# Routed experts in units of 32 rows in four column lanes, with the gate weights copied by ScalarE, in place of units of 64 rows in two lanes

## The chip, the cores and the metric

The kernel runs on one core of one Trainium2 chip. The metric is the device time of one execution in microseconds (us); the lower the better. TensorE is written PE, VectorE DVE, ScalarE ACT, GpSimd POOL, and SP is the engine that issues most DMAs. All tensors are 32-bit floats.

## The reference

One layer of a decoder: 256 prompt tokens and 64 sample tokens pass a native-sparse-attention block with a gating unit, a memory cross-attention and, last, a mixture of experts, whose part is what the change touches:

```python
def hier_moe(h, w_rg, w_re, w_gate, w_up, w_down):     # h: 320 tokens x 2048
    pg = softmax(xf @ w_rg); g_top = argmax(pg)        # one of 4 groups
    fl = (xf @ w_re)[group g_top]; pf = softmax(fl)    # 4 experts of that group
    top_p, top_i = top_k(pf, 2)                        # two experts per token
    wts = top_p / sum(top_p) * max(pg)
    act = silu(xf @ w_gate[e]) * (xf @ w_up[e])        # 2048 -> 512, each of 16 experts
    act = act * comb[:, e]                             # weight of expert e for the token, or 0
    return sum over e of act @ w_down[e]               # 512 -> 2048
x = x + hier_moe(rmsnorm(x, g_moe_norm), ...);  y = rmsnorm(x, g_final)
```

Every expert has three weight matrices of 4.19 MB (gate, up, down); the 16 experts have 201 MB. 320 tokens with two experts each are 640 pairs. The reference's router, evaluated on the reference's own inputs, gives experts 0 to 15 these numbers of pairs: 15, 38, 32, 51, 86, 64, 52, 30, 44, 62, 77, 29, 4, 20, 15, 21. In units of 64 rows that is 18 units (experts 4 and 10 have two, all others one). In units of 32 rows it is 26: experts 4 and 10 have three, experts 1, 3, 5, 6, 8 and 9 two, the other eight one.

## The kernel before

The program is a sequence of stages, each a block in which all engines run their own instruction lists and meet at semaphores. The last block is the expert stage (line 2408 on). Just before it, a short block (line 2239) makes the routing table on DVE: how many units there are, which expert each has, and which token stands in each row of it.

The expert stage is a loop over units, called turns. In one turn PE

- turns the rows of the next unit, which POOL has gathered from memory with an indirect DMA (`turn_rows`, L2473);
- multiplies this unit's activation with the down weights (`down`, transposes L2510, matmuls L2517: 16 matmuls of 512 columns);
- multiplies the next unit's rows with gate and up weights (`gate_up`, L2499 and L2500: 16 chunks of 128 input features; gate fills output rows 0 to 63 and up rows 64 to 127 of one bank, side by side in two lanes of 64 columns of the array);
- between chunks of gate_up, sends the previous unit's result rows back to their tokens with a one-hot matrix (`move`, L2487, five times), which DVE adds to x (L2595).

[...]

ACT applies silu (L2550), copies the turned activation for `down` (L2552) and half of the result (L2554). DVE multiplies gate by up and by the routing weight (L2579) and copies the other half (L2589).

Weights are in SBUF in buffers of 4.19 MB. There is one buffer for up (`w_u`), one for down (`w_d`) and three for gate, taken in turn by expert number (`gate_unit`). Each matrix is loaded in four quarters of 1.05 MB, and SP issues them in one order in each turn: up of this turn's expert (L2419), gate of the expert two ahead (L2430), down of this turn's expert (L2424). A quarter of up waits on `gu_used[q]`, that is until PE's gate_up of the turn before has used that quarter; a quarter of down waits likewise on `d_used[q]`. A turn with the same expert as the one before issues the same waits, and its transfers are switched off by a condition (`cond=`). The gates of experts 0, 1 and 2 (L1822, L1828), up 0 (L2244) and down 0 (L2247) are loaded ahead of the stage. All of them go through SP's one queue, in the order of issue.

## Time and profile before

| | |
|---|---|
| median of 3 runs | 1599.32 us (1598.54 to 1600.5) |
| the profiled execution | 1600.59 us, its span 1598.7 us |
| expert stage in the span | 1048.7 us to the end |
| PE busy in the whole span | 1470.7 us (92%) |
| mean granted PE clock | 0.956 |
| moved by DMA | 361.20 MB |

The span is the time between the first and the last instruction that the profiler saw; 1.9 us of the execution lie outside it. [...]

### The profile page before, as it was taken

To read this page: it belongs to the slowest core of one execution; us is meant where nothing else is said; L and a number is where in the kernel's file an instruction comes from. 1 tells how busy PE (TensorE), PEld (TensorE's weight loads), DVE (VectorE), ACT (ScalarE), POOL (GpSimd) and SP (SyncE) were. 2 spreads that over 40 slices of the span, in tenths; PEclk is the share of its full clock that TensorE was granted. 3 is DMA by queue.
4 is the path that set the end of the run, shared out by engine and by line. 5 is a ranking of instruction groups with operands and counts; after the bars stand their busy time and mean duration, and the time that the engine had idled before them with its cause. 6 is when DMAs were issued, how large, how long until landed. Compare 5 with 4: busy or idle time off the path is not lost. (4 is left out here: it accounts for less than half of the span.)

```text
span 1598.7 us, 21805 instructions
## 1 busy us (share of the span) xinstructions
PE 1470.7 (92%) x8104; PEld 848.5 (53%) x8105; DVE 608.2 (38%) x1162; ACT 316.0 (20%) x702; POOL 43.7 (3%) x55
## 2 busy tenths in 40 slices
PE   7999999998999798778999999769999999999994
PEld 4478887777888566544444565523333333333331
DVE  3154333432654365466100303523343333433335
ACT  3001011222333144366000203101001010010102
POOL 0000000003000000000000000000000000000000
PEclk9999999999999699798999999879999999999998
DMA  9254537434530377202844024979987999969981
GB/s 348 105 172 160 198 134 261 148 134 149 195 113 7 119 238 236 67 1 89 297 152 164 1 106 155 410 261 419 421 360 274 421 421 422 410 251 421 421 311 66
DMA packets 108867, 361.20 MB, mean 226 GB/s; under 512 B 16600, under 2 KB 44288, under 8 KB 80482
## 3 DMA queue, kind: packets, MB, share of 16 engines
q1 hardware_dynamic: 104546, 329.63, 54.5%
q0 software_dynamic: 3744, 22.43, 3.8%
q10 hardware_dynamic: 512, 8.26, 1.4%
q8 instruction: 43, 0.70, 0.2%
q14 instruction: 22, 0.18, 0.0%
HBM read 388.83 MB, written 17.05 MB: 254 GB/s over the span
## 5 line engine op out<-in xcount | busy, mean ns | idle before, releaser
L2499 PE MATMUL bank<-ring,hT_e 128*64 x576 | 267.1, 603 | 1.8 <-DVE hT_e L2574 1.8
L2500 PE MATMUL bank<-ring,hT_e 128*64 128x512 f32 x576 | 267.1, 603 | 0.0
L2595 DVE TENSOR_TENSOR x<-x,bank 128x1024 f32<-128x1024 f32 (+1 forms) x108 | 131.5, 1220 | 213.2 <-PE bank L2487 210.1
L2499 PEld LDWEIGHTS bank<-ring,hT_e 128*64 128x64 f32 x576 | 73.8, 137 | 179.5 <-issue 179.4
L2517 PE MATMUL bank<-W,const 128*64 128x512 f32 x576 | 127.6, 595 | 11.6 <-ACT const L2552 11.6
L1855 PE MATMUL bank<-W,mixT 128*128 128x512 f32 x256 | 113.4, 604 | 1.6 <-DVE mixT L2090 1.6
L2487 PE MATMUL bank<-const,own_rows 64*128 64x512 f32 (+1 forms) x408 | 95.3, 632 | 0.0
L2517 PEld LDWEIGHTS bank<-W,const 128*64 128x64 f32 x576 | 41.1, 137 | 84.6 <-issue 84.1
L1855 PEld LDWEIGHTS bank<-W,mixT 128*128 128x128 f32 x256 | 49.1, 193 | 63.5 <-issue 61.4
L2500 PEld LDWEIGHTS bank<-ring,hT_e 128*64 128x64 f32 x576 | 73.7, 137 | 0.0
L2550 ACT ACTIVATE gate<-bank 64x512 f32<-64x512 f32 x18 | 10.6, 588 | 307.6 <-PE bank L2500 307.6
L515 PE MATMUL bank<-raw,hT 128*128 128x256 f32 (+1 forms) x288 | 65.2, 384 | 0.0
L524 PE MATMUL bank<-raw,hT 128*64 128x256 f32 (+1 forms) x576 | 64.8, 383 | 0.0
L515 PE MATMUL bank<-w_in,hT 128*128 128x256 f32 (+1 forms) x288 | 64.3, 380 | 0.0
L2487 PEld LDWEIGHTS bank<-const,own_rows 64*128 64x128 f32 (+1 forms) x408 | 24.0, 167 | 69.0 <-issue 69.0
L515 PEld LDWEIGHTS bank<-raw,hT 128*128 128x128 f32 x288 | 54.0, 190 | 11.1 <-issue 3.5
L515 PEld LDWEIGHTS bank<-w_in,hT 128*128 128x128 f32 x288 | 54.5, 189 | 8.4
L524 PEld LDWEIGHTS bank<-raw,hT 128*64 128x64 f32 x576 | 40.6, 137 | 21.7 <-issue 1.4
L864 PE MATMUL bank<-const,rawg 128*128 128x128 f32 (+1 forms) x320 | 48.0, 273 | 4.0 <-ACT rawg L924 4.0
L2099 DVE TENSOR_TENSOR x<-bank,x 128x512 f32<-128x512 f32 x16 | 11.0, 690 | 98.9 <-PE bank L1855 98.9
L976 DVE TENSOR_TENSOR d_even<-bank,x_odd 128x256 f32<-128x256 f32 x64 | 27.1, 424 | 51.9 <-ACT x_odd L933 51.5
L864 PEld LDWEIGHTS bank<-const,rawg 128*128 128x128 f32 (+1 forms) x320 | 39.4, 151 | 13.3 <-ACT rawg L924 4.1
(425 smaller groups left out, 2029.5 us busy)
## 6 DMA issues: line engine op xcount, KB each, us to landing
ring<-in_w_exp_gate SPq DMA_DIRECT2D x80, 1024.0 KB
ring<-in_w_exp_up SPq DMA_DIRECT2D x72, 1024.0 KB
W<-in_w_exp_down SPq DMA_DIRECT2D x72, 1024.0 KB
raw<-in_w_in SPq DMA_DIRECT2D x10, 2048.0 KB
raw<-in_w_in SPq DMA_DIRECT2D x8, 2096.0 KB
W<-in_w_out SPq DMA_DIRECT2D x3, 4096.0 KB, 13.6
k_in<-in_cache_sel_k SPq DMA_DIRECT2D x64, 128.0 KB
v_in<-in_cache_sel_v SPq DMA_DIRECT2D x64, 128.0 KB, 3.3
```

Source lines behind the costliest of these rows:

```text
L515: mm = pe.matmul(to, left(c), right(c), start=(start and c == 0), stop=(c == 7), skip_group_check=True)
L524: mm = pe.matmul(b[64 * h:64 * h + 64, :], hT[:, c, 2 * P:2 * P + NS], w[:, c, h * half:(h + 1) * half], start=(c == 0), stop=(c == KC - 1))
L864: mm = pe.transpose(bank[k % LEAD][:, g * n:g * n + n], rawg[0:n, q // 4, a:a + P], ident[0:n, 0:n])
L976: dve.tensor_tensor(d_even[:, k % LEAD, :].rearrange("p (k m) -> p k m", m=HALF), x, odd, ALU.subtract)
L1855: mm = pe.matmul(to, hT[:, c, r * P:r * P + P], w(c, slice(0, 512)), start=(c == 0), stop=(c == chunks - 1))
L2099: dve.tensor_tensor(cols, to, cols, ALU.add).then_inc(added, 1)
L2487: mm = pe.matmul(bank2[to][rows, 512 * (n % 2):512 * (n % 2) + 512], own_rows[lane, P * r:min(P * r + P, TOK)], y[lane, n // 2, :], start= ...
L2499: pe.matmul(GATE[0:NS, :], hT[:, c, :], w_g[:, c, :], start=(c == 0), stop=(c == KC - 1))
L2500: mm = pe.matmul(GATE[UP, :], hT[:, c, :], w_u[:, c, :], start=(c == 0), stop=(c == KC - 1))
L2517: mm = pe.matmul(bank[n // 2][LANES[n % 2], :], actT[:, q, :], w_d[:, q, 512 * n:512 * n + 512], start=(q == 0), stop=(q == 3))
L2550: act.activation(gate[UP, :], GATE[0:NS, :], ACT.Silu).then_inc(silu_ready, 1)
L2595: ins = dve.tensor_tensor(x[0:rows, r, cols], x[0:rows, r, cols], src, ALU.add)
```

## The change

Experts are processed in units of 32 rows. A unit's rows fill one lane of 32 columns of the array, and there are four lanes: for gate_up two of them take the two halves (256 columns each) of gate, the other two those of up; for `down` each takes 512 of the 2048 output columns. So a chunk of gate_up is four matmuls of 256 columns in place of two of 512. In `move` the four lanes are row groups of 32, with 512 columns each into four banks; there are three moves in a turn, one for each tile of tokens.

PE reads gate weights from a fixed buffer, `w_g` (unit 0 of the ring). ACT copies them there, in four quarters for each turn, from one of two buffers into which the gates are loaded (`gate_slot`). SP's order in a turn stays up, gate, down, but the gate is that of the next expert, not of the one after it, and the gate of expert 2 is no longer loaded ahead of the stage. The halves of the gathered rows become quarters, and the layout of the weights' rows over partitions follows. The table that the routing block makes has 38 columns in place of 28.

```diff
-TURNS_MAX = NE + 2 * (SEQ + NS) // NS
+UNIT = 32
+UNITS_EACH = TOK // UNIT
+TURNS_MAX = NE + 2 * TOK // UNIT
...
+        w_g = ring[:, 0, :].rearrange("p (c n) -> p c n", n=FF)
...
-        def gate_unit(e):
-            return (e * 2 + 2) % 3 * 2
+        def gate_slot(e):
+            return e % 2 * 2 + 2
 
         quarter = lambda q: slice(4 * q, 4 * q + 4)
 
         def gate_loads(e):
-            g = A["w_exp_gate"][0, bass.ds(e, 1)].rearrange("o (h p c) f -> (o p) h c f", h=2, p=P)
-            w_g = ring[:, bass.ds(gate_unit(e), 1), :].rearrange("p o (c n) -> p (o c) n", n=FF)
-            return [(w_g[:, quarter(q), :], g[:, q // 2, quarter(q % 2), :]) for q in range(4)]
+            g = A["w_exp_gate"][0, bass.ds(e, 1)].rearrange("o (h p c) f -> (o p) h c f", h=4, p=P)
+            held = ring[:, bass.ds(gate_slot(e), 1), :].rearrange("p o (c n) -> p (o c) n", n=FF)
+            return [(held[:, quarter(q), :], g[:, q]) for q in range(4)]
 
         def up_loads(e):
-            up = A["w_exp_up"][0, bass.ds(e, 1)].rearrange("o (h p c) f -> (o p) h c f", h=2, p=P)
-            return [(w_u[:, quarter(q), :], up[:, q // 2, quarter(q % 2), :]) for q in range(4)]
+            up = A["w_exp_up"][0, bass.ds(e, 1)].rearrange("o (h p c) f -> (o p) h c f", h=4, p=P)
+            return [(w_u[:, quarter(q), :], up[:, q]) for q in range(4)]
 
         def down_loads(e):
-            d = A["w_exp_down"][0, bass.ds(e, 1)].rearrange("o (p c) n -> (o p) c n", c=4)
-            return [(w_d[:, q, :], d[:, q, :]) for q in range(4)]
+            d = A["w_exp_down"][0, bass.ds(e, 1)].rearrange("o (h p c) n -> (o p) h c n", h=2, p=P)
+            return [(w_d[:, q, :], d[:, q // 2, q % 2, :]) for q in range(4)]
...
-                        if r == 2:
-                            sp.wait_ge(made, 24)
-                            for q, load in enumerate(gate_loads(2)):
-                                sp.wait_ge(g_loaded[q], 32)
-                                sp.dma_start(*load).then_inc(g_loaded[q], 16)
...
-                    dve.tensor_scalar(ahead[:, :], owner_f[:, :], 1.0, float(NE - 1), ALU.add, ALU.min)
-                    L(dve.tensor_tensor(past[:, :, :], rank[:, 0, :].unsqueeze(2).to_broadcast([P, PAIRS, 4]),
-                                        cst("tile_over")[:, 1:5].unsqueeze(1).to_broadcast([P, PAIRS, 4]), ALU.is_ge))
+                    dve.tensor_scalar(ahead[:, :], owner_f[:, :], float(NE - 1), None, ALU.min)
...
-            UP = slice(NS, P)
-            LANES = [slice(0, NS), UP]
-            y = const[:, P:P + 1024].rearrange("p (h n) -> p h n", h=2)
-            rows_in = const[:, P + 1024:P + 2048]
-            actT = const[:, P + 2048:P + 2048 + 4 * NS].rearrange("p (k r) -> p k r", k=4)
-            pe_passed, slot_ready, h_turned, h_copied, silu_ready, act_ready, a_turned, a_copied, y_copied_a, y_copied_d = (
+            UP = slice(P // 2, P)
+            LANES = [slice(UNIT * n, UNIT * n + UNIT) for n in range(4)]
+            y = const[:, P:P + 512]
+            rows_in = const[:, P + 512:P + 1024]
+            actT = const[:, P + 1024:P + 1024 + 4 * UNIT].rearrange("p (c h r) -> p c h r", c=2, h=2)
...
-            GATE, ACT_T, ROWS_B = bank[4], bank[5], (bank[6], bank[7])
-
-
-            MOVES = [(0, 0, 1), (0, 1, 0), (1, 0, 1), (1, 1, 0), (2, None, 1)]
-            LAST_BANKS = {0: (1, 0), 1: (2, 3), 2: (1, 1)}
-            MOVE_AFTER = {2: 0, 6: 1, 10: 2, 13: 3, 15: 4}
+            gf = ring[:, gate_slot(NE - 2), 0:D]
+            GATE, DOWN, ROWS_B, ACT_T = bank[4], bank[5], bank[6], bank[7]
+            TILE_ROWS = [P, P, NS]
+            MOVE_AFTER = {3: 0, 10: 1, 15: 2}
...
-                            sp.wait_ge(g_loaded[q], turn * 16 + 32)
+                            sp.wait_ge(g_loaded[q], turn * 16 + 16)
+                            sp.wait_ge(g_copied[q], turn)
                             sp.dma_start(dst, src, cond=(following > before)).then_inc(g_loaded[q], 16)
...
+                        for k in range(4):
+                            mm = pe.transpose(ROWS_B[:, k * P:k * P + P], rows_in[:, k:512:4], ident)
+                        mm.then_inc(h_turned, 1)
...
+                    def move(turn, r):
+                        if r == 0:
+                            pe.wait_ge(own_ready, turn + 1)
+                            pe.wait_ge(y_copied, turn + 1)
+                        pe.wait_ge(added, turn * 3 + r + 3)
                         pe.sem_inc(pe_passed, 1)
-                        for k in range(8):
-                            for h, lane in enumerate(LANES):
-                                mm = pe.transpose(ROWS_B[h][:, k * NS:k * NS + NS], rows_in[lane, k:1024:8], ident[lane, lane])
-                        mm.then_inc(h_turned, 1)
-
-                    def move(turn, k):
-                        r, half, to = MOVES[k]
-                        if k == 0:
-                            pe.wait_ge(own_ready, turn + 1)
-                            pe.wait_ge(y_copied_a, turn + 1)
-                            pe.wait_ge(y_copied_d, turn + 1)
-                        pe.wait_ge(added, turn * 5 + k + 4)
-                        pe.sem_inc(pe_passed, 1)
-                        for n in range(4) if half is None else (2 * half, 2 * half + 1):
-                            lane = LANES[n % 2]
-                            rows = slice(0, P) if r < 2 else LANES[n // 2]
-                            mm = pe.matmul(bank2[to][rows, 512 * (n % 2):512 * (n % 2) + 512], own_rows[lane, P * r:min(P * r + P, TOK)],
-                                           y[lane, n // 2, :], start=True, stop=True)
+                        for n, lane in enumerate(LANES):
+                            mm = pe.matmul(bank[n][0:TILE_ROWS[r], :], own_rows[lane, P * r:P * r + TILE_ROWS[r]], y[lane, :], start=True, stop=True)
                         mm.then_inc(moved, 1)
 
-                    def gate_up(turn, e, moving=None):
-                        w_g = ring[:, bass.ds(gate_unit(e), 1), :].rearrange("p o (c n) -> p (o c) n", n=FF)
-                        pe.wait_ge(h_copied, turn * 2 + 2)
+                    def gate_up(turn, moving=None):
+                        pe.wait_ge(h_copied, turn + 1)
                         for q in range(4):
-                            pe.wait_ge(g_loaded[q], turn * 16 + 16)
+                            pe.wait_ge(g_copied[q], turn + 1)
                             pe.wait_ge(u_loaded[q], turn * 16 + 16)
                             pe.sem_inc(pe_passed, 1)
-                            for c in range(4 * q, 4 * q + 4):
-                                pe.matmul(GATE[0:NS, :], hT[:, c, :], w_g[:, c, :], start=(c == 0), stop=(c == KC - 1))
-                                mm = pe.matmul(GATE[UP, :], hT[:, c, :], w_u[:, c, :], start=(c == 0), stop=(c == KC - 1))
-                                if c == 4 * q + 3:
+                            for k in range(4):
+                                c = 4 * q + k
+                                for n, lane in enumerate(LANES):
+                                    cols = slice(256 * (n % 2), 256 * (n % 2) + 256)
+                                    mm = pe.matmul(GATE[lane, 0:256], hT[:, k, q, :], (w_g if n < 2 else w_u)[:, c, cols], start=(c == 0), stop=(c == KC - 1))
+                                if k == 3:
                                     mm.then_inc(gu_used[q], 1)
...
+                        for c in range(2):
+                            mm = pe.transpose(ACT_T[:, c * 2 * UNIT:(c + 1) * 2 * UNIT], gate[UP, c:256:2], ident[UP, UP])
                         mm.then_inc(a_turned, 1)
                         pe.wait_ge(a_copied, turn + 1)
-                        pe.wait_ge(added, turn * 5 + 4)
                         for q in range(4):
                             pe.wait_ge(d_loaded[q], turn * 16 + 16)
-                            for n in range(4):
-                                mm = pe.matmul(bank[n // 2][LANES[n % 2], :], actT[:, q, :], w_d[:, q, 512 * n:512 * n + 512], start=(q == 0), stop=(q == 3))
+                            for n, lane in enumerate(LANES):
+                                mm = pe.matmul(DOWN[lane, :], actT[:, q % 2, q // 2, :], w_d[:, q, 512 * n:512 * n + 512], start=(q == 0), stop=(q == 3))
                             mm.then_inc(d_used[q], 1)
...
+                        gate_up(turn + 1, turn)
...
+                    def copy_gate(turn, q):
+                        held = ring[:, bass.ds(gate_slot(expert_of(turn)), 1), :].rearrange("p o (c n) -> p (o c) n", n=FF)
+                        act.wait_ge(g_loaded[q], turn * 16 + 16)
+                        act.copy(w_g[:, quarter(q), :], held[:, quarter(q), :]).then_inc(g_copied[q], 1)
+
+                    def activate(turn):
                         act.wait_ge(gu_used[3], turn + 1)
-                        act.activation(gate[UP, :], GATE[0:NS, :], ACT.Silu).then_inc(silu_ready, 1)
+                        act.activation(gate[UP, :], GATE[0:P // 2, 0:256], ACT.Silu).then_inc(silu_ready, 1)
+
+                    def keep_act(turn):
                         act.wait_ge(a_turned, turn + 1)
-                        act.copy(actT, ACT_T[:, 0:4 * NS].rearrange("p (k r) -> p k r", k=4)).then_inc(a_copied, 1)
+                        act.copy(actT, ACT_T[:, 0:4 * UNIT].rearrange("p (c h r) -> p c h r", c=2, h=2)).then_inc(a_copied, 1)
+
+                    def keep_y(turn):
                         act.wait_ge(d_used[3], turn + 1)
-                        act.copy(y[:, 0, :], bank[0]).then_inc(y_copied_a, 1)
-
-                    with act.Fori(0, count(act, 0)) as turn:
-                        step(turn)
+                        act.copy(y, DOWN).then_inc(y_copied, 1)
+
+                    expert_of = lambda turn: act.value_load(experts[0:1, bass.ds(turn, 1)], min_val=0, max_val=NE - 1)
+                    for q in range(4):
+                        copy_gate(0, q)
+                    last = count(act, 1)
+                    with act.Fori(0, last) as turn:
+                        activate(turn)
+                        copy_gate(turn + 1, 0)
+                        keep_act(turn)
+                        copy_gate(turn + 1, 1)
+                        copy_gate(turn + 1, 2)
+                        keep_y(turn)
+                        copy_gate(turn + 1, 3)
+                    activate(last)
+                    keep_act(last)
+                    keep_y(last)
...
+                    def add(turn, r):
+                        dve.wait_ge(moved, turn * 3 + r + 1)
+                        add_tile(r, bank2[0:2]).then_inc(added, 1)
```

PE's loop body stands thus in the kernel before (its names: `ring` holds the weights, `hT_e` the turned rows, `own_rows` the one-hot matrix; the columns are the source line, the operation with output and inputs, and the shape):

```order
L2510 MATMUL bank_2<-const,gate 128x64 x4
L2513 ISA
L2515 ISA
L2517 MATMUL bank_0<-W,const 64x512 x16
L2493 ISA
L2499 ISA
L2499 REGISTER_ALU
L2499 MATMUL bank_2<-ring,hT_e 64x512
L2500 MATMUL bank_2<-ring,hT_e 64x512
```

and thus in the changed kernel, where the last rows are those up to the second move:

```order
L2501 MATMUL bank_3<-const,gate 128x64 x2
L2505 ISA
L2507 MATMUL bank_2<-W,const 32x512 x16
L2482 REGISTER_ALU
L2491 MATMUL bank_2<-ring,hT_e 32x256 x16
L2475 ISA
L2478 MATMUL bank_0<-const,own_rows 128x512 x2
L2478 MATMUL bank_1<-const,own_rows 128x512 x2
L2491 MATMUL bank_2<-ring,hT_e 32x256 x28
L2475 REGISTER_ALU
L2478 MATMUL bank_0<-const,own_rows 128x512 x2
L2478 MATMUL bank_1<-const,own_rows 128x512 x2
```

The two matmuls of a chunk, 512 columns wide in tiles of 64, became four, 256 wide in tiles of 32 (16 instructions for the four chunks ahead of the first move); a move became four matmuls.

ACT's loop body before:

```order
L2550 ACT_TABLE_LOAD
L2550 ACTIVATE gate<-bank_2 64x512
L2552 COPY const<-bank_2 128x256
L2554 COPY const<-bank_0 128x512
```

and in the changed kernel (from the silu on; TENSOR_LOAD reads a unit's expert number into a register):

```order
L2538 ACTIVATE gate<-bank_2 64x256
L2548 ISA
L2548 TENSOR_LOAD experts
L2548 ISA x2
L2533 ISA
L2534 ISA
L2534 COPY ring<-ring 128x2048
L2542 COPY const<-bank_3 128x128
```

A copy of a gate quarter (L2534) now stands between the silu and the copy of the turned activation (L2542); two more follow before the result's copy, and one behind it.

## Rows read from the trace of the kernel before

**Rows 1.** Windows (us from:to, length, busy per engine, PE clock, DMA share, GB/s), expert stage.
```profile
1000.00:1050.00 50.00, 31.71 (x260) 23.11 (x258) 28.66 (x99) 8.23 (x24) 0.74 (x2) 0.79 1.01 413
1100.00:1180.00 80.00, 78.05 (x394) 26.36 (x396) 29.61 (x32) 8.49 (x12) 3.61 (x6) 1.00 1.01 421
1192.00:1205.00 13.00, 12.36 (x57) 4.11 (x58) 5.02 (x7) 2.24 (x3) 1.02 (x1) 1.00 0.17 50
1205.00:1221.00 16.00, 15.84 (x86) 5.30 (x82) 5.54 (x5) 0.71 (x2) 0.18 (x1) 1.00 0.68 214
```
**Rows 2.** Groups by line and form, window 1050 to 1600 us.
```profile
L2500 PE MATMUL bank<-ring,hT_e 128*64 128x512 f32 x576 | 267.1, 603 | 0.0
L2517 PE MATMUL bank<-W,const 128*64 128x512 f32 x576 | 127.6, 595 | 11.6 <-ACT const L2552 11.6
L2595 DVE TENSOR_TENSOR x<-x,bank 128x1024 f32<-128x1024 f32 x72 | 87.6, 1221 | 212.4 <-PE bank L2487 210.1 <-PE bank L2542 2.4
```
**Rows 3.** Timeline of ACT: one turn, and the last of the stage.
```profile
1131.79 0.59 ACT L2550 ACTIVATE gate<-bank 64x512 f32<-64x512 f32 x1 [16.69 <-PE bank L2500]
1134.31 0.37 ACT L2552 COPY const<-bank 128x256 f32<-128x256 f32 x1 [1.93 <-PE bank L2510]
1142.07 0.58 ACT L2554 COPY const<-bank 128x512 f32<-128x512 f32 x1 [7.39 <-PE bank L2517]
1160.65 0.59 ACT L2550 ACTIVATE gate<-bank 64x512 f32<-64x512 f32 x1 [16.69 <-PE bank L2500]
...
1574.41 0.58 ACT L2554 COPY const<-bank 128x512 f32<-128x512 f32 x1 [7.37 <-PE bank L2517]
```
**Rows 4.** Waits of SP's queue, 1050 to 1560 us: total, times, longest.
```profile
SPq L2419 <- PE bank L2500: 254.7, 68, 13.6
```
**Rows 5.** DMA queue of POOL's gathers (MB), and median time to landing, 1050 to 1560 us.
```profile
q0 software_dynamic: 2592, 5.65, 3.1%
...
const<-scratch_hn,from_row POOLq DMA_INDIRECT x18, 8.1
```
**Rows 6.** Timeline from the landing of the first gather on, PE and SP.
```profile
1055.06 1.15 PE L2473 MATMUL bank<-const 64*128 64x64 f32 x16 [8.09 <-DMA const<-scratch_hn,from_row]
...
1058.02 1.09 PE L2499 MATMUL bank<-ring,hT_e 128*64 x1 [1.80 <-DVE hT_e L2574]
...
1060.60 1.06 PE L2499 MATMUL bank<-ring,hT_e 128*64 x1
...
1063.47 0.59 PE L2499 MATMUL bank<-ring,hT_e 128*64 x1
...
1063.90 0.59 PE L2499 MATMUL bank<-ring,hT_e 128*64 x1
...
1064.41 0.37 SPq L2419 DMA_DIRECT2D ring<-in_w_exp_up  x1
```
**Rows 7.** Windows of 1 us behind that first issue.
```profile
1065.00:1066.00 1.00, 1.00 (x6) 0.31 (x4) 0.00 (x0) 0.00 (x0) 0.00 (x0) 1.00 0.60 106
1066.00:1067.00 1.00, 1.00 (x8) 0.40 (x6) 0.00 (x0) 0.00 (x0) 0.00 (x0) 1.00 0.93 254
1067.00:1068.00 1.00, 1.00 (x8) 0.37 (x6) 0.00 (x0) 0.00 (x0) 0.00 (x0) 1.00 0.88 369
1068.00:1069.00 1.00, 1.00 (x6) 0.31 (x4) 0.00 (x0) 0.00 (x0) 0.00 (x0) 1.00 1.23 393
```
**Rows 8.** Timeline of PE: matmuls in four lanes of 32 columns, in the memory attention.
```profile
989.47 3.19 PE L1949 MATMUL bank<-W,mix 128*32 128x512 f32 x28
```
**Rows 9.** Timeline: a move, the last moves, and a pass of ACT over 2048 elements.
```profile
1124.96 1.13 PE L2487 MATMUL bank<-const,own_rows 64*128 64x512 f32 x4
...
1575.46 3.70 PE L2542 MATMUL bank<-const,own_rows 64*128 64x512 f32 x16 [1.09 <-DVE const L2589]
...
1579.87 1.91 ACT L2563 ACTIVATE W<-x 128x2048 f32<-128x2048 f32 x1 [4.87 <-DVE x L2595]
```
**Rows 10.** A window of the attention stage, columns as in Rows 1.
```profile
672.00:686.00 14.00, 8.49 (x34) 5.23 (x34) 11.09 (x48) 6.03 (x24) 0.00 (x0) 0.50 0.00 1
```

More of the change, by code:

```diff
@@ L2219, in trunk @@
             wts = side(scope, "wts", [P, TILES, 2])
-            over = side(scope, "over", [P, NE, 5])
+            over = side(scope, "over", [P, NE, UNITS_EACH])
             tiles = side(scope, "tiles", [P, NE])
@@ L2412, in _ @@
                     expert_of = lambda turn: sp.value_load(experts[0:1, bass.ds(turn, 1)], min_val=0, max_val=NE - 1)
[L2413 removed]
+                    ahead_of = lambda turn: sp.value_load(ahead[0:1, bass.ds(turn, 1)], min_val=1, max_val=NE - 1)
                     n = count(sp, 0)
@@ L2611, in _ @@
                     drain(1)
-                    keep_y(0)
-                    for k in range(4):
-                        add(0, k)
+                    add(0, 0)
+                    add(0, 1)
                     last = count(dve, 1)
```

131 lines of the change are left out of this document (55 added, 76 removed).

## The prediction

> **What bounds the kernel now.** I read the windows of the expert stage first. In a long stretch PE is busy 78.05 of 80 us at the full clock and the DMA engines move 421 GB/s with a share of 1.01 [rows 1]: PE and the weight stream are both full. Which of them sets the pace is told by the turns: silu starts at 1131.79 and 1160.65, 28.9 us apart, and from the result's copy at 1142.07 to the last one at 1574.41 there are 15 turns of 28.82 us [rows 3]. One expert's weights, 12.58 MB, take 29.9 us at 421 GB/s, more than a turn. A stage paced by DMA would therefore show PE waiting for transfers; its matmul rows name ACT as what ended their idle time, 11.6 us in sum, and no DMA [rows 2]. SP, on the other hand, waits 254.7 us in 68 waits for PE to use up the buffer of up weights [rows 4]. So PE sets the pace, and the stream keeps up only because three gates are loaded ahead of the stage and because in an extra turn of an expert (the second one of experts 4 and 10) it can catch up; there DMA falls to 50 GB/s and then 214 [rows 1]. The reader is to see that the stream has a margin of only about a turn and that PE cannot become much faster before the stream is the bound.
>
> The reference's router needs 18 units of 64 rows, or 26 of 32.
>
> **PE's work after.** Work out one unit of 32 rows that waits for nothing.
> - gate_up. At the full clock two lanes start a record every 0.43 us (1063.47, 1063.90), and each 512-column matmul is two records [rows 6]: 0.855 us a chunk, 13.7 us a turn. Four lanes run side by side elsewhere in this kernel: 28 records of 512 columns in tiles of 32 take 3.19 us, 0.114 us each, a quarter of 0.43 [rows 8]. With 256 columns a chunk is 8 records of half that, 0.43 us; 16 chunks are 6.8 us.
> - down. 32 records in four lanes: 32 x 0.107 = 3.4 us, against 7.1 (127.6 us of busy records, 32 a turn in two lanes) [rows 2].
> - moves. A move in row lanes now costs 1.13 us [rows 9]. Two of the three stand inside gate_up: 2.3 us. DVE's two adds of 1.22 us behind each [rows 2] must be done before the next move overwrites the banks; 7 chunks (3.0 us) stand between, so little is lost, 0.3 us.
> - from the end of gate_up to the first down matmul. Now 1131.75 to 1134.68 (end of ACT's copy), 2.9 us [rows 3]. A new copy of 2048 elements stands ahead of that copy on ACT; the nearest row is 1.91 us for a pass over 2048 elements [rows 9]. DVE's product, the transposes and the third move (1.1 us) run beside it. Silu 0.4, reading the expert number, the copy 1.9 and ACT's small copy 0.3 give 3.1 to 3.5; I take 3.3. ACT's whole load is about 11 us a unit, under 16, and its other three copies find cover in down and gate_up.
>
> Sum 6.8 + 3.4 + 2.6 + 3.3 = 16.1 us, or 26 x 16.1 = 419 us against 18 x 28.83 = 519. If PE were still the bound, 100 us would go.
>
> **The weight stream after.** It does not let them go.
> - Bytes. In the stage there are 15 up, 15 down and 14 gate matrices (gate 2 is now among them): 44 x 4.19 = 184.5 MB. The gathers bring 5.65 MB [rows 5], the same data as after. 190.2 MB at 421 GB/s are 451.7 us.
> - Begin. The first up is issued at 1064.41 [rows 6]. The first quarter of gate_up began at 1058.02 at the half clock (three records to 1060.60, 0.86 us each, in place of 0.43) and took 6.4 us; in four lanes it is 4 x 0.86 = 3.4 us, 3.0 less. The gather ahead of it has one matrix less in the queue (landing then nearer to the shortest of these gathers, 1.3 us less, in my estimate), one multiply on DVE is 0.6 less, and the wider routing table costs about 1.5 us on DVE and PE. First issue at about 1061.0. Its 1.05 MB were in SBUF at 1068.8, 4.4 us after the issue, since the rate starts at 106 and 254 GB/s [rows 7]; at 421 they take 2.5. So a restart of the idle stream costs 1.9 us, and the stream counts from 1062.9.
> - Idle time at a change of expert behind an extra unit. There is still one buffer for up. The last unit of an expert can begin gate_up only after the unit before it has done `down`, whose weights are last in SP's order. So the stream stands idle from the landing of down until PE has done the last quarter of down (0.9 us) and the first of gate_up (1.7), then restarts (1.9), and its next three quarters are issued at PE's pace (two moves among them), 0.5 us slower than it could take them: 5.0 us. Eight experts have extra units: 40 us.
> - A third unit. Experts 4 and 10 have three units, and the stream stands still for the whole middle one: 2 x 16.1 = 32 us.
> - End. 1062.9 + 451.7 + 72.2 + 0.9 (last quarter of down) = 1587.7.
>
> Before, the last down ended at 1574.4 [rows 3]. That is 13.3 us later. Behind it the final moves in four row lanes deliver the first tile after 0.9 us in place of 1.8 (3.70 us for 16 records [rows 9]), 0.9 us less, and the rest of the tail is the same DVE and ACT work. Total 1600.6 + 13.3 - 0.9 = 1613.0 on the profiled execution's own time, which lies 1.3 us over the median of the runs: **1612 us**, slower by 0.8%.
>
> What the removed parts give: two moves, the result's copy on DVE and PE's reading of the expert number lie beside the stream and are worth nothing. What covers the added ACT copies (104 x 1.9 us) is the same waiting; in a unit that does not wait they cost 0.4 us in the chain above. The copies wait for gates, but SP issues gate ahead of down, so ACT's first copy never holds `down` longer than down's own weights do.
>
> Bounds of the unknown terms. The restart: a stream that never drained would lose 0, a full 1.9 each; eight times: -15 to 0. A copy from SBUF to SBUF: from 0.58 us (512 elements from PSUM, rows 3) times one to four times that, 2.3: between -1.3 and +0.4 us for a unit, which counts only for the two middle units. Four lanes at 0.114 in place of 0.107: 0.5 us a unit, +5 over the ten extra units. The gather in the stream's way: with or without it, 13 us less (5.65 MB at 421) or 0. PE's clock: the second rival.
>
> [...]
>
> **The rivals.**
> 1. The stream hands over faster, and PE's saving shows (other side: faster). Place: the eight changes of expert. If the first up quarter follows with no restart loss and the pacing costs nothing, a change costs 2.6 us in place of 5.0 (-19 us), and if gathers fit into gaps of the stream that exist anyway, another 5 are gone: 1612 - 24 = 1588. It decides once the idle time sums to under 60 us (72.2 - 12.4). For it: DMA ran at 422 in windows with gathers too, so that gathers may use otherwise idle slots. Against it: in the extra turn before, with PE busy throughout, the stream needed 1205 to 1221 at 214 GB/s for one matrix [rows 1]: an up that PE paces is a slow one.
> 2. [...] PE will be busy some 16 of 30 us beside single-unit experts, waiting up to 7 us in one piece. In the attention stage 8.49 busy of 14 us went with a clock of 0.50 throughout [rows 10]; after the idle time before 1058 dense matmuls still ran at the half clock at 1060.6 and at the full one by 1063.5 [rows 6]. While PE follows the stream this is hidden (a quarter of gate_up 3.4 us against 2.5 for its load: gate_up ends later, yet ahead of down's landing). At a change behind an extra unit it is not: 0.9 more for down, 1.7 for the quarter, about 0.5 for what follows, 3 us, eight times: 1612 + 24 = 1636. With a middle unit at the half clock too, 1655.
> [...]
> 3. Four lanes don't overlap as far as [rows 8] says, because a chunk now has 16 PE instructions (8 loads of weights, 8 matmuls) in 0.43 us. At 0.55 a chunk a unit is 1.9 us longer; the stream's path has the first quarter at eight changes and two middle units: +8 us, 1620. At no overlap (1.7 us a chunk) it would be over 1900; rows 8 exclude that.
> 4. The change does less than it says: the number of units is data, and if a count stands on the other side of 32 (expert 2 has just 32 pairs) one unit more comes: +5 us.
>
> **How the numbers follow.** Forecast 0.50, with its own range 1600 to 1624; rival 1 0.20; rival 2 0.18; rivals 3 and 4 together 0.12. The range of 8 in 10 goes from 1590, near rival 1, to 1640, past rival 2. What a measurement can tell from no change here is 0.2%, 3.2 us. Faster: most of rival 1, 0.17. Within 0.2% (1596.1 to 1602.5): the rest of it and the lower end of the forecast, 0.11. Slower 0.72.
>
> **What the profile after would show.** Windows with 421 GB/s while PE is busy just over half; PE rows that wait for the DMAs of up and down, over 100 us in sum, where none waits now. Silu intervals of three kinds: about 16 us inside an expert, 20 to 22 at its next unit, 30.7 through the single-unit experts at the end (11 to 15). Chunk records of L2491 in steps of 0.43 us for eight. GB/s near zero for some 20 us in the third units. Copies on ACT near 1.9 us. The forecast is wrong if PE's waits for DMA stay under 60 us, if silu intervals at the end are under 29, or if the last down ends before 1575.

## The result: 1644 us, slower by 2.7%, and the profile after

The changed kernel takes 1644.02 us (median; 1642.71 to 1645.75), the kernel before 1599.91 beside it; the ratio is 1.0273, interval 1.0254 to 1.0292. I had forecast 1612, in a range that ended at 1640. The direction and the bound are as forecast (the weight stream in place of PE). The size is not.

Where it is visible first is the windows of the expert stage (columns as in [rows 1]). The first two lie in the last, single-unit experts. The next two are changes of expert behind a second unit, and the fifth is the middle unit of expert 4.

```profile
1500.00:1550.00 50.00, 38.18 (x346) 12.91 (x350) 12.13 (x13) 14.30 (x12) 1.21 (x2) 0.70 1.01 421
1550.00:1600.00 50.00, 32.95 (x268) 9.89 (x260) 13.18 (x15) 17.16 (x15) 1.21 (x2) 0.73 1.01 421
...
1257.00:1265.00 8.00, 7.65 (x88) 2.58 (x84) 1.49 (x2) 3.77 (x3) 0.00 (x0) 0.78 0.18 56
...
1408.00:1417.00 9.00, 8.32 (x80) 2.75 (x76) 1.03 (x1) 3.77 (x3) 0.00 (x0) 0.66 0.14 49
...
1200.00:1225.00 25.00, 23.16 (x270) 9.71 (x270) 9.76 (x11) 13.58 (x11) 1.21 (x2) 0.88 0.09 25
```

Where the stream runs it runs full, at 421 GB/s, with PE busy in part only (33 to 38 of 50 us). In the other windows it stands nearly still, and there PE is busy: PE works while the stream is empty, and waits while it is full. Windows of 1 us show eight such stretches in the stage. Counted as the sum of (1 - GB/s / 421.5) over their windows, they lose 8.0, 7.8, 6.9, 7.4, 8.0 and 8.0 us at the six experts with two units, and 23.5 and 22.3 at the two with three.

The groups that answer to [rows 2], and what PE waits for between 1050 and 1600 us (engine, line waited for: total, times, longest):

```profile
L2507 PE MATMUL bank<-W,const 128*32 128x512 f32 x832 | 145.9, 813 | 94.3 <-DMA W<-in_w_exp_down 85.0
L2491 PE MATMUL bank<-ring,hT_e 128*32 128x256 f32 x3328 | 210.9, 403 | 5.5 <-DMA ring<-in_w_exp_up 4.6
L2534 ACT COPY ring<-ring 128x2048 f32 x104 | 194.7, 1897 | 37.6 <-issue 22.7
```
```profile
PEld bank L2507 <- DMA W<-in_w_exp_down: 151.6, 56, 6.0
...
PE bank L2507 <- DMA W<-in_w_exp_down: 82.7, 56, 5.8
...
PE bank L2491 <- DMA ring<-in_w_exp_up: 4.6, 6, 0.8
```

104 copies on ACT at 1.90 us are as priced. Nearly all the waits are for down weights, the last of the three matrices in SP's order; 4.6 us are for up. The matmuls that follow them are the long ones: 813 ns a record on average. In experiment 5 below, which hardly waits for down, the same line has 595. The trace has two records for each matmul of L2507 and L2491: 832 for 16 matmuls in each of 26 units, and 3328 for 64 in each; [rows 2] has 576 of L2500 for 16 in each of 18 units.

Silu in the changed kernel comes 16.1 us apart wherever nothing is waited for (11 of 25 intervals), 22.9 to 28.5 at the second unit of each expert that has one (it follows the first one's wait for down weights), and 30.6 at two of the single-unit experts near the end. The other four intervals are 26.2 to 27.7, the last one of the stage among them. The forecast had 16, 20 to 22, and 30.7.

### The profile page after: what moved, and what is told of

Read it like the earlier page. It is cut to its first block and busy times, and to the rows that moved or that the text cites. A ratio compares the mean times of both kernels' runs of the same rounds, so it can differ in the third digit from the quotient of the medians.

```text
span 1641.9 us, 27729 instructions
## 1 busy us (share of the span) xinstructions
PE 1424.6 (87%) x10524; PEld 853.9 (52%) x10524; DVE 641.5 (39%) x1198; ACT 520.0 (32%) x838; POOL 53.6 (3%) x71
## 2 busy tenths in 40 slices
DMA packets 108676, 360.96 MB, mean 220 GB/s; under 512 B 16462, under 2 KB 44150, under 8 KB 80290
## 5 line engine op out<-in xcount | busy, mean ns | idle before, releaser
L2595 DVE TENSOR_TENSOR x<-x,bank 128x1024 f32<-128x1024 f32 x156 | 183.2, 1215 | 335.5 <-PE bank L2478 328.0
L2507 PE MATMUL bank<-W,const 128*32 128x512 f32 x832 | 145.9, 813 | 94.3 <-DMA W<-in_w_exp_down 85.0
L2491 PE MATMUL bank<-ring,hT_e 128*32 128x256 f32 x3328 | 210.9, 403 | 5.5 <-DMA ring<-in_w_exp_up 4.6
L2534 ACT COPY ring<-ring 128x2048 f32 x104 | 194.7, 1897 | 37.6 <-issue 22.7
L2491 PEld LDWEIGHTS bank<-ring,hT_e 128*32 128x32 f32 x3328 | 109.4, 116 | 138.0 <-issue 85.7
L2507 PEld LDWEIGHTS bank<-W,const 128*32 128x32 f32 x832 | 22.4, 124 | 186.8 <-DMA W<-in_w_exp_down 156.1
L2478 PE MATMUL bank<-const,own_rows 32*128 32x512 f32 (+1 forms) x600 | 86.6, 646 | 6.8 <-DVE x L2595 6.8
L2538 ACT ACTIVATE gate<-bank 64x256 f32<-64x256 f32 x26 | 9.8, 375 | 163.3 <-PE bank L2491 163.3
L2546 ACT COPY const<-bank 128x512 f32<-128x512 f32 x26 | 15.2, 584 | 128.9 <-PE bank L2507 128.9
L2009 ACT ACTIVATE o_mT<-x 128x512 f32<-128x512 f32 (+1 forms) x12 | 7.6, 630 | 137.4 <-DVE x L2097 111.6
```

What stands on the lines that cost most here:

```text
L2478: mm = pe.matmul(bank[n][0:TILE_ROWS[r], :], own_rows[lane, P * r:P * r + TILE_ROWS[r]], y[lane, :], start=True, stop=True)
L2491: mm = pe.matmul(GATE[lane, 0:256], hT[:, k, q, :], (w_g if n < 2 else w_u)[:, c, cols], start=(c == 0), stop=(c == KC - 1))
L2507: mm = pe.matmul(DOWN[lane, :], actT[:, q % 2, q // 2, :], w_d[:, q, 512 * n:512 * n + 512], start=(q == 0), stop=(q == 3))
L2534: act.copy(w_g[:, quarter(q), :], held[:, quarter(q), :]).then_inc(g_copied[q], 1)
L2595: ins = dve.tensor_tensor(x[rows, r, cols], x[rows, r, cols], src[rows, :], ALU.add)
```

## Experiments

They vary the order of SP's three loads, by what the waits are counted, ACT's order, and the work on PE beside its waits. "Gaps" are the lost microseconds of the stream at the changes of expert, worked out as above; the first six values in a row are the experts with two units. All ratios are to the kernel before on the same chip.

| kernel | time (us) | ratio and interval | last silu in the stage (us) |
|---|---|---|---|
| the change as it is | 1644.0 | 1.0273 (1.0254 to 1.0292) | 1609.2 |
| 1: down ahead of gate | 1641.2 | 1.0272 (1.0247 to 1.0297) | 1602.2 |
| 2: PE kept at work in all units | 1660.0 | 1.0378 (1.0361 to 1.0395) | 1627.0 |
| 3: kernel before, gate one ahead | 1599.7 | 1.0005 (0.9991 to 1.0018) | - |
| 4: 1 and ACT's order | 1608.9 | 1.0059 (1.0042 to 1.0076) | 1580.2 |
| 5: 4, waits and loads by expert | 1570.7 | 0.9814 (0.9792 to 0.9836) | 1540.6 |
| 6: the change, waits and loads by expert | 1641.1 | 1.0257 (1.0233 to 1.0281) | 1600.7 |
| 7: the change, ACT's order alone | 1642.1 | 1.0277 (1.0252 to 1.0301) | 1606.2 |
| 8: PE kept at work in first units | 1691.1 | 1.0566 (1.0536 to 1.0596) | 1655.2 |
| 9: 5 without ACT's order | 1575.9 | 0.9843 (0.9815 to 0.9871) | 1541.8 |

**1. Down ahead of the next gate.**
```diff
                         load_up(turn, e, previous)
-                        load_gate_ahead(turn)
                         load_down(turn, e, previous)
+                        load_gate_ahead(turn)
```


> The changed kernel with one edit: SP issues up, down, gate of the next expert in place of up, gate, down. Theory A (the loss is idle time of the weight stream: it drains behind down and restarts only when PE has done the last quarter of down and the first of gate_up; eight times some 9 us, and 16 us for each of two middle units): the gate of the next expert now streams for 10 us while PE does that, so the eight gaps close and the two long ones shrink to under 10 us. Idle of the stream in the stage from 104 us to under 40, time 1644 - 65 = 1579, within 1565 to 1595. Theory B (PE's own time at the half clock is what costs): the clock drops as often as before, so the time moves by less than 15 us, 1630 to 1644. Theory C (the stream is slower because of ACT's copies or the gathers, and not idle): no change beyond 5 us.

Measured 1641.2, no gain; the gaps are 10.0, 8.0, 7.8, 9.3, 8.3, 8.8 and 24.3, 23.5. The timeline of ACT and PE at one of them (start, length, engine, line, in brackets the idle time before and what ended it) says why:

```profile
1280.86 0.38 ACT L2538 ACTIVATE gate<-bank 64x256 f32<-64x256 f32 x1 [5.36 <-PE bank L2491]
...
1287.05 1.90 ACT L2534 COPY ring<-ring 128x2048 f32 x1 [5.82 <-DMA ring<-in_w_exp_gate]
1288.86 0.26 ACT L2542 COPY const<-bank 128x128 f32<-128x128 f32 x1
...
1289.25 6.27 PE L2507 MATMUL bank<-W,const 128*32 128x512 f32 x32 [6.03 <-ACT const L2542]
```

The first gate copy stands on ACT ahead of the activation copy L2542 (the `keep_act` that `down` needs). It waits 5.8 us for a gate, and PE's `down` waits behind it. The gate was that of the *next expert*, though the next unit is of the same one: `g_loaded` is counted by turns. So this run didn't test what I meant, since the wait moved from down to gate. The time lies in the range that theory B (the half clock) had, but not for its reason: the granted clock (TensorE's, as a share of its full one) over the six gaps is 0.92 to 1.00 here, against 0.66 to 0.78 in the changed kernel, and they are no shorter.

**2. PE kept at work.** Two matmuls of 256 columns ahead of each quarter's wait in `down`, in every unit.
```diff
                         for q in range(4):
+                            for _ in range(2):
+                                pe.matmul(ACT_T[:, 256:512], ident, cst("before"), start=True, stop=True)
                             pe.wait_ge(d_loaded[q], turn * 16 + 16)
```


> The changed kernel with 8 more matmuls of 256 columns a unit, two ahead of each wait for a quarter of down, into a part of a bank that nobody reads: they keep PE busy while it waits. They cost 8 x 0.43 = 3.4 us in a unit that waits for nothing. Theory B (the half clock makes up most of the loss at a change of expert): the clock stays at 1.0 through the waits, each of the eight gaps in the stream gets 4 us shorter, 1644 - 32 + 7 (two middle units) = 1619. Theory A (the clock is the smaller part: 0.85 us for the last quarter of down and 0.8 for the first of gate_up): gaps 1.7 us shorter, 1644 - 14 + 7 = 1637. If the clock has no share at all: 1651.

Measured 1660.0, over all three expected times. The stage's window from 1100 to 1500 and the added group:

```profile
1100.00:1500.00 400.00, 371.31 (x3843) 169.06 (x3846) 160.07 (x171) 184.19 (x150) 23.02 (x38) 0.98 0.75 302
```
```profile
L2506 PE MATMUL bank<-const 128*128 128x256 f32 x416 | 122.0, 417 | 17.6 <-ACT const L2544 17.6
```

The clock was held (0.98), yet a unit that waits for nothing took 20.7 us, 4.6 more, and PE became the bound at 302 GB/s. The gaps stayed at 6.7 to 8.8 and 29. The run doesn't price the half clock, because the cover cost more; it does show that a full clock alone doesn't close the gaps.

**3. The kernel before, with the gate one expert ahead** (and gate 2 not loaded ahead of the stage).
```diff
-                    dve.tensor_scalar(ahead[:, :], owner_f[:, :], 1.0, float(NE - 1), ALU.add, ALU.min)
+                    dve.tensor_scalar(ahead[:, :], owner_f[:, :], float(NE - 1), None, ALU.min)
...
-                            sp.wait_ge(g_loaded[q], turn * 16 + 32)
+                            sp.wait_ge(g_loaded[q], turn * 16 + 16)
```


> The kernel before with one part of the change alone: the gate that SP loads in a turn is the next expert's and not the one after it, and the gate of expert 2 is not loaded ahead of the stage. Units of 64 rows and two lanes stay. If the shallower prefetch alone makes the stream the bound (30.7 us for an expert with the gathers against 28.8 for a turn, with about 10 us less in hand), PE waits up to 2 us a turn in runs of single turns: 1600 + 0 to 8. If the depth of the prefetch is what the change lost (a rival to theory A), 1625 or more.

Measured 1599.7 against 1598.6, no difference. Its wait for weights in the whole stage:

```profile
PEld bank L2512 <- DMA W<-in_w_exp_down: 0.5, 1, 0.5
```

In the kernel before, the third gate buffer, which the change gives up, was worth nothing. What it would be worth in the changed kernel, where the stream is the bound, no run shows. There PE waits for down weights and not for a gate.

**4. Down ahead of gate, and ACT's `keep_act` ahead of its first gate copy.** Experiment 1 with ACT's loop as:
```diff
-                        copy_gate(turn + 1, 0)
                         keep_act(turn)
+                        copy_gate(turn + 1, 0)
                         copy_gate(turn + 1, 1)
-                        copy_gate(turn + 1, 2)
                         keep_y(turn)
+                        copy_gate(turn + 1, 2)
                         copy_gate(turn + 1, 3)
```


> As the kernel with SP's order up, down, gate, and besides ACT's first copy of a gate quarter stands behind its copy of the turned activation, not ahead of it. Theory: once the stream's gaps are closed, two units of 16.1 us are longer than an expert's 30.7 us of stream, so PE's chain counts again; without the 1.9 us copy in it a unit takes 14.8 us, and the time is 6 to 12 us under that kernel's. If the stream is the only bound: less than 3 us.

Measured 1608.9, 32 us less than 1, where 6 to 12 were expected. The gaps fall to 4.8 to 6.0 and some 20, but don't close. What ACT waits for, one of the gaps, and ACT and PE just ahead of it and in it:

```profile
ACT ring L2534 <- DMA ring<-in_w_exp_gate: 84.6, 49, 6.4
```
```profile
1283.00:1289.00 6.00, 6.00 (x70) 2.48 (x64) 2.35 (x2) 4.39 (x3) 0.00 (x0) 0.72 0.18 63
```
```profile
1276.63 1.90 ACT L2534 COPY ring<-ring 128x2048 f32 x1 [3.91 <-DMA ring<-in_w_exp_gate]
...
1278.63 1.93 PE L2491 MATMUL bank<-ring,hT_e 128*32 128x256 f32 x32 [2.14 <-issue]
...
1282.60 1.26 PE L2478 MATMUL bank<-const,own_rows 32*128 32x512 f32 x8 [2.04 <-ACT const L2546]
```

The copies still wait 85 us for gates, and PE's gate_up waits behind them: it starts as the first copy ends, and its first move waits for the result's copy, L2546, which stands behind the second. That is where I formed the theory that the following runs test: the loads are handed over late because a repeated unit waits for a gate that it doesn't use.

**5. Loads and waits by expert.** SP's loop is written out over the experts, without the turns that issue nothing; PE and ACT wait for the count of their expert, not of their turn. Order up, down, gate; ACT as in 4.
```diff
-                    with sp.Fori(1, n) as turn:
-                        e, previous = expert_of(turn), expert_of(turn - 1)
-                        load_up(turn, e, previous)
...
+                    for e in range(1, NE):
+                        first = sp.value_load(firsts[0:1, e:e + 1], min_val=e, max_val=TURNS_MAX)
+                        for q, (dst, src) in enumerate(up_loads(e)):
+                            sp.wait_ge(u_loaded[q], e * 16)
+                            sp.wait_ge(gu_used[q], first)
+                            sp.dma_start(dst, src).then_inc(u_loaded[q], 16)
...
-                        act.wait_ge(g_loaded[q], turn * 16 + 16)
+                        act.wait_ge(g_loaded[q], e * 16 + 16)
```


> The changed kernel with SP's loop written out over the 15 experts (no turns that issue nothing), each transfer issued in the order up, down, gate of the next, every wait for weights counted by expert instead of by turn, and ACT's copies behind keep_act and keep_y as they come free. Theory A (a change of expert costs 9.1 us because its loads are handed over one by one behind waits that are not for the buffer they go to: up waits for the last quarter of up, while down's quarters stand behind it and behind the next gate, and a second unit waits for the next expert's gate): the idle time of the stream at each of the eight changes falls from 7 to 8 us to under 3, that of the two middle changes from 23 to some 12 to 18; the kernel takes 1565 to 1585 us. Rival B (the time is TensorE's and its half clock: the units are 16.1 us and the last ones 30.6, whatever the order of the loads): 1600 to 1635, with the same eight gaps or TensorE late beside them. Rival C (the stream's order is of no matter, only SP's turn is): 1625 to 1640.

Measured 1570.7, ratio 0.9814: faster than both kernels, and within theory A's range. Four windows (the second and the third are the middle-unit gaps), then what PE and ACT wait for, then ACT's last copy:

```profile
1110.00:1186.00 76.00, 61.78 (x756) 27.05 (x756) 33.75 (x36) 38.76 (x32) 4.86 (x8) 0.93 1.01 421
1186.00:1201.00 15.00, 14.30 (x182) 6.21 (x178) 7.73 (x9) 8.90 (x8) 1.22 (x2) 1.00 0.23 74
...
1388.00:1403.00 15.00, 14.30 (x182) 6.23 (x178) 7.62 (x9) 8.91 (x8) 1.21 (x2) 1.00 0.17 53
...
1240.00:1388.00 148.00, 132.26 (x1631) 57.84 (x1635) 71.46 (x78) 86.03 (x71) 10.75 (x17) 0.95 1.01 416
```
```profile
PE bank L2482 <- DMA ring<-in_w_exp_up: 64.1, 6, 12.1
...
ACT ring L2527 <- DMA ring<-in_w_exp_gate: 36.5, 23, 5.6
```
```profile
1548.18 0.59 ACT L2539 COPY const<-bank 128x512 f32<-128x512 f32 x1 [5.41 <-PE bank L2498]
```

From 1240 to 1388 us four experts with two units (5, 6, 8 and 9) and one with a single unit pass, and the stream holds 416 GB/s throughout; the longest losses of the stage are 12.4 and 13.1 us, in the middle units. The gaps at the six experts with two units are gone, and silu comes every 15.8 us in 17 of 25 intervals. The last result copy stands at 1548.2, 69.6 us earlier than in the changed kernel.

**6. Loads and waits by expert, in the order up, gate, down**, ACT as in the changed kernel (the diff of 5 with `load_down`'s part last).

> The same loop over experts and the same counting, but the order up, gate of the next, down and ACT's order as in the changed kernel. Separates SP's way through turns that issue nothing, and the waits counted by turn, from the order itself. Theory A: down still stands behind up's wait, so the eight gaps shrink only by SP's own share (0.5 to 1 us each) and the kernel takes 1632 to 1642 us. Rival C (SP's turns are the cost): each gap loses 2 us or more and the kernel takes 1615 to 1628.

Measured 1641.1, no different from the change. The six gaps are 8.0, 6.5, 6.5, 7.7, 6.8 and 7.1, the two middle ones 23.1 and 23.4. One of them:

```profile
1289.00:1298.00 9.00, 7.81 (x80) 2.94 (x80) 1.33 (x2) 3.77 (x3) 0.00 (x0) 0.68 0.19 59
```

The mean of the six is 7.1 us against 7.7 in the changed kernel: the loop over experts takes 0.6 us from a gap at most. Part of that is the execution that was profiled, which took 1634.3 us, 7 under the median, and had a granted clock of 0.79 to 0.81 in three of its gaps. Where down is last, the stream has nothing left while PE works off down and begins the next gate_up.

**7. ACT's order alone** (the diff of 4 on the changed kernel).

> The changed kernel with one edit: ACT makes keep_act ahead of the first gate copy and keep_y ahead of the last two. Tells how much of the change's cost is the copies of ScalarE standing ahead of what TensorE waits for. Theory A: nothing waits for ACT at a change of expert in this order (the gate has landed long before), so only the repeated units gain: 1638 to 1643 us, eight gaps as before. Rival D (the copies are on the path in every unit, 1.9 us each time): 16.1 us units become 14.5 to 15 and the kernel takes 1610 to 1630.

Measured 1642.1: no gain. Units that wait for nothing take 15.8 us in place of 16.1, so the first gate copy costs 0.3 us on the chain there, and the six gaps stay at 6.8 to 8.5 us, with the same wait for down behind them.

```profile
PEld bank L2507 <- DMA W<-in_w_exp_down: 158.5, 56, 7.7
```

**8. PE kept at work in first units only.** Three matmuls ahead of quarters 1 to 3 in `down`, switched by a table of first units.
```diff
                         for q in range(4):
+                            if q:
+                                with pe.Fori(0, k):
+                                    for _ in range(3):
+                                        pe.matmul(ACT_T[:, 256:512], ident, cst("before"), start=True, stop=True)
                             pe.wait_ge(d_loaded[q], turn * 16 + 16)
```


> The changed kernel with three small matmuls (128 x 256) ahead of the second, third and fourth quarter's wait in down, only in the first unit of an expert, so that TensorE works while the stream is waited for and repeated units are left alone. Theory A (clock worth 0.8 us, up to 1.7, of each change): 1630 to 1640 us, gaps 6.5 to 7.5 us. Rival E (the half clock makes the difference between 5.0 and 9.1 us): gaps of 5 us and less, the last units under 29 us, 1605 to 1618. If the added work itself delays the quarters: over 1645.

Measured 1691.1: in the third of the expected cases, the one over 1645 in which the added work itself delays the quarters. The group of the added matmuls and a gap:

```profile
L2513 PE MATMUL bank<-const 128*128 128x256 f32 x468 | 141.1, 444 | 0.0
```
```profile
1395.00:1404.00 9.00, 9.00 (x96) 4.54 (x96) 1.14 (x1) 3.73 (x3) 0.00 (x0) 1.00 0.08 20
```

468 records are 234 matmuls at two each, as in experiment 2 (416 for 208), or 9 in each of 26 units: they ran in every unit, not in the first ones alone (whether the table or a loop over zero steps did that was not looked into), and silu came 21.8 or 23.4 us apart. The run isn't the one its expectation describes. It repeats what 2 showed: at a granted clock of 0.89 to 1.00 over the six gaps (1.00 in the one above) the stream still stands for 8.5 to 13.0 us at a change, now with the added matmuls ahead of the quarters.

**9. As 5, with ACT's order of the changed kernel.**

> The loop over experts in the order up, down, gate of the next, with waits counted by expert, but with ACT's order as in the changed kernel (the first gate copy ahead of keep_act). Tells whether the 1570.7 us came from the counting or also needed ACT's order. Theory A1 (the copy ahead of keep_act waits for the next gate at every change of expert, since that gate is now the last of the three loads, so ACT holds down and with it the next loads): gaps of 6 to 9 us come back at the eight changes, the middle ones stay near 13; 1610 to 1635 us. Theory A2 (with waits by expert the gate is always early enough): within 3 us of 1570.7.

Measured 1575.9, ratio 0.9843; 5 us over the median of 5, where theory A2 allowed 3, and the intervals overlap. So ACT's order, worth 32 us between 1 and 4, is worth some 5 at most once waits go by expert. PE's waits for ACT and ACT's for gates, against 108.0 and 117.8 us in run 1:

```profile
PE bank L2498 <- ACT const L2535: 60.7, 26, 10.6
...
ACT ring L2527 <- DMA ring<-in_w_exp_gate: 52.3, 18, 10.4
```

## Why the prediction was wrong

**What held.** The bound moved to the stream, at 421 GB/s. The unit that waits for nothing takes 16.1 us, as summed. Experts 13 and 14 take 30.6 us each (forecast 30.7), the last one 27.7. PE's waits for down pass 60 us, and the last unit was later than 1575. The bytes are right: 185.61 MB on SP's queue and 5.12 of gathers between 1050 and 1620 us, 190.73 in sum, against 190.2.

**What failed: the term "idle time at a change of expert behind an extra unit", put at 5.0 us.** The last down ended at 1617.8, the copy that follows it (next row), where the forecast had 1587.7: 30.1 us. The first up was issued at 1056.0 and not 1061.0, which makes 5.0 less. So the idle terms are 35 us over the 72.2. The tail was 24.1 us, where 23.4 was forecast: of the 0.9 us that the final moves were to save, 0.2 came. 30.1 + 0.7 is, but for rounding, the difference of 30.7 to the profiled execution's 1643.7.

```profile
1617.77 0.58 ACT L2546 COPY const<-bank 128x512 f32<-128x512 f32 x1 [6.60 <-PE bank L2507]
```

One change in full, in the second unit of expert 6: first the last two quarters of down and what follows, PE and SP; then the DMA engines' rate in slices of 0.5 us from 1290 on.

```profile
1296.12 1.94 PE L2507 MATMUL bank<-W,const 128*32 128x512 f32 x8 [1.40 <-DMA W<-in_w_exp_down]
...
1298.40 1.93 PE L2507 MATMUL bank<-W,const 128*32 128x512 f32 x8 [0.34 <-DMA W<-in_w_exp_down]
...
1300.11 2.56 PE L2491 MATMUL bank<-ring,hT_e 128*32 128x256 f32 x32
...
1302.60 1.14 PE L2478 MATMUL bank<-const,own_rows 32*128 32x512 f32 x8
...
1303.03 3.23 SPq L2415 DMA_DIRECT2D ring<-in_w_exp_up  x2
```
```profile
GB/s 426 459 377 475 360 442 451 401 401 393 434 377 410 311 197 33 0 0 0 0 0 0 0 0 0 0 0 0 98 197 377 475 393 410 361 98 377 459 459 377
```

The full rate ends at about 1297.3, the last bytes come by 1297.7, and PE takes up the last quarter at 1298.40: 1.1 us that the sum didn't have. The quarter takes 1.7 us to the start of gate_up, where 0.9 stood; gate_up's first quarter 2.5, where 1.7 stood. SP issues 0.4 us behind it. The first bytes come at 1304.0, 1.0 us on, and the ramp costs another 0.7: the restart is 1.7 us, where 1.9 stood. The sum is 7.4, and this gap was counted as 7.4; the mean of the six is 7.7.

The other five gaps show the same at both ends: 0.7 to 0.8 us from the last bytes to PE's start, 0.9 to 1.0 from the issue to the first bytes. The pace that follows, while up is issued as PE uses up its quarters, was put at 0.5. Windows of 1 us show 1.4 to 2.0 us lost in the 12 us behind each of the eight gaps, 1.8 in the mean.

The sum over the stage agrees. From 1056.0 to 1617.2 the stream had 561.2 us for bytes that take 452.5, so it lost 108.7. The eight stretches hold 91.9 of them, start and end 1.9 + 2.0, and 12.9, or 1.6 for each change, are left for the pace. So a change costs some 9.2 us in place of 5.0, and over eight changes that is 34 of the 35 us.

I had taken what a transfer costs beside its bytes as the cost of a restart alone. The trace of SP's loads shows time at both ends, with no more of it behind the bytes than ahead of them: 0.7 us from the last bytes to PE's start, and 1.0 from the issue to the first ones.

**The half clock, rival 2, is the largest single part of what was missing, and under half of it.** What a quarter of down and the first quarter of gate_up take at the full clock (granted clock 1.00) stands in the first three rows; the fourth is the change that lost the least.

```profile
1614.17 1.07 PE L2507 MATMUL bank<-W,const 128*32 128x512 f32 x8 [0.94 <-DMA W<-in_w_exp_down]
...
1276.57 1.92 PE L2491 MATMUL bank<-ring,hT_e 128*32 128x256 f32 x32
1278.41 1.14 PE L2478 MATMUL bank<-const,own_rows 32*128 32x512 f32 x8
...
1260.46 1.91 PE L2491 MATMUL bank<-ring,hT_e 128*32 128x256 f32 x32
```

The last quarter of down ran at the half level in all six changes (granted clock 0.50): 1.7 us in place of 0.9. The first quarter of gate_up took 1.85 to 3.04 us up to its first move, 2.5 in the mean, in place of 1.84 (1276.57 to 1278.41), since the clock came back within it or just ahead of it: in the change above the granted clock was 0.50 over the last quarter and 0.73 over the first one, and at 1260.46 it was 1.00. That is 0.8 to 2.0 us for a change, 1.5 in the mean, or some 12 of the 34 us. Rival 2 had priced 3 us, with the whole first quarter at the half level. The other terms that I had missed or put too low are the landing (1.1), the pace (1.1 to 1.3) and SP (0.4).

The gaps themselves say the same. The changed kernel and experiments 6 and 7 have 18 of them with two-unit experts. The 7 with a granted clock of 0.78 or more lost 6.5 to 7.0 us, the 11 with 0.74 or less lost 7.1 to 8.5: 1.1 us between the means. So a full clock would shorten the gaps and not close them; experiment 1 had 7.8 us and more with 0.92 to 1.00, and 2 and 8 had 6.7 and more, though in these three PE was late for other reasons. Rival 2's 1636 came near the time by another sum. No run held the clock without adding work.

The clock was not at the half level behind every wait for weights: the last down quarter took 1.93 us for its eight records, at a granted clock of 0.50, in the change above, but the one at 1614.17, behind a wait of 0.94 us, took 1.07, at 1.00. And the price is only paid where PE is on the stream's path, and that is two quarters in each change.

**Rival 1's place was right, its sign wrong.** The handover at the eight changes decides the time, and I had looked for a gain there with the three loads in their given order. The experiments show that the cost isn't in the changes as such. In order up, gate, down the last load is the one on which PE's chain to the next up hangs, so each change pays landing, last quarter, first quarter and restart in one line. In order up, down, gate the next gate (10 us of stream) can cover that chain. But ACT's first gate copy then stands in front of what PE needs and, counted by turn, waits in a second unit for the next expert's gate, so the chain is as long as before (1).

The new order of loads gives nothing alone (1641.2), and neither do the other two edits alone, waits and loads by expert (1641.1) and ACT's order (1642.1). With ACT's order beside it, it gives 35 us (4); with waits and loads by expert 68 (9); with both 73 (5). So ACT's order takes half of the way; the other half, and the closing of the gaps, needed waits that ask only for what a unit uses. The prediction held all three fixed, and I didn't ask whether the sum of idle times was due to the data's dependence or to the count.

**What stays open.** Loads by expert and SP's shorter loop came in one edit; 6 bounds the two together at a few us in the old order, but in the new order they weren't taken apart. The middle units still lose 12.4 and 13.1 us. The forecast put the standing of the stream there down to the one buffer for up, and no run had a second one.

## What to carry to other kernels

When a change turns a compute-bound loop into a stream-bound one, write the chain from the last byte of one group to the first byte of the next, with both ends of the DMA in it (here 1.1 us for the landing and 1.7 for the restart), and ask which load in the order could cover it. Check what each wait counts: a semaphore counted by iteration also asks for transfers that this iteration doesn't use, and that shows only when the order of the loads is changed. A reordering that gives nothing alone may be the missing half; look at which engine now waits for which transfer before dropping it.

## What the runs showed of the hardware

- For quarters of 1.05 MB, 0.7 to 0.8 us lay between the last bytes in the rate and the start of the matmul that waited for them, and 0.9 to 1.0 between the issue and the first bytes of the idle stream (six changes of the changed kernel).
- Keeping PE at work has its price in full: 208 matmuls of 128x256 kept PE busy for 122.0 us, 0.59 each (the trace has 416 records for them, of 417 ns, which overlap in part), and eight of them lengthened a unit by 4.6 us and the kernel by 16 (experiment 2).
- The page's line on HBM reads counts transfers that were switched off. The first row is the changed kernel's, the second that of experiment 5; their queues moved 360.96 and 360.98 MB.

```profile
HBM read 482.68 MB, written 17.05 MB: 304 GB/s over the span
```
```profile
HBM read 352.66 MB, written 17.05 MB: 235 GB/s over the span
```

The difference is 130.0 MB, or 31 matrices of 4.19 MB: the 30 that the ten repeated units switch off, and one gate at the end. In the gaps the rate is near zero, so they weren't read. The line is not a measure of traffic where loads have a condition.
